# Feed-forward of a prompt and a sample group: the prompt in 512-column matmuls, the sample tokens as stationary operand in four column groups

## The chip, the cores and the metric

One Trainium2 chip, one of its cores. The metric is the device time of one launch in microseconds (us); the shown time before is the median of three runs.

## The reference, cut to what matters

Two groups of tokens run through the same two-layer trunk with the same weights: a prompt of 1024 tokens and 8 x 4 = 32 sample tokens. Each layer has a mixer (layer 0 convolutions, layer 1 attention) and then the feed-forward part, which is what the change touches (cut, with `D_MODEL` = 1024 and `D_FF` = 2816):

```python
def causal_dwconv(x, state, w):           # width 3; returns the last 2 input rows as new state
    xp = jnp.concatenate([state, x], axis=1)
    ...
def conv_ffn(h, st, w_in, wc, w_down):
    z = h @ w_in
    g, st_new = causal_dwconv(z[..., :D_FF], st, wc)
    return (jax.nn.silu(g) * z[..., D_FF:]) @ w_down, st_new
...
    fp, nfp = conv_ffn(rms_norm(hp, g_ffn[layer]), zf, w_ffn_in[layer], conv_f_w[layer], w_down[layer])
    fs, nfs = conv_ffn(rms_norm(hs, g_ffn[layer]), state_ffn[layer], w_ffn_in[layer], conv_f_w[layer], w_down[layer])
    hp = hp + fp
    hs = hs + fs
```

All data are fp32.

## The kernel before

Activations lie transposed: channels on the 128 partitions, tokens along the row, the 1024 prompt tokens first and the 32 sample tokens behind them (`T` = 1056). A matmul takes a 128x128 block of weights as stationary operand and streams tokens. The 1056 tokens are three pieces of 352 (`NT` = 3, `TS` = 352), each into a PSUM bank of its own; the two regions `reg[0]` and `reg[1]` have three banks each and alternate from use to use (`region(use)`).

Precision comes from splitting: every fp32 value is a rounded part (type fp32r, one pass of TensorE) and a rest. ScalarE makes the rounded part of a unit of weights (`split_hi`, line 381), GpSimd the rest (`split_lo`, line 386), and each product is taken as high*high, high*low, low*high. So one block of 128x128 weights against all tokens is 3 x 3 = 9 matmuls of 352 columns.

Weights come as a stream of units of 128x1024 values (512 KB). `w_raw` has three slots for what was loaded, `w_sp` three for the split parts. SyncE's queue loads unit u once `w_lo` says that the unit in the same slot, u-3, was split (`load_unit`, line 374); it also issues the copies of the caches (`copy_piece`, 4 MB each). The split of unit u+3 is made when TensorE has finished unit u (`hi_after`, `lo_after`).

The feed-forward part of a layer (`ffn(L)`) has 11 groups of 256 hidden channels. A group has four units of the input projection (gate and up of two chunks of 128 channels; `in_proj`, line 626, 72 matmuls a unit) and two units of the down projection (`down_proj`, line 677, 72 matmuls a unit in four uses of 18). The down projection of group g-1 stands behind the input units of group g. Its first two input units go with `first_units`, which puts between them the sums for the norm's factor: VectorE takes reciprocals (lines 1535 and 1537) into `rst`, with which every result of the input projection is multiplied when it leaves PSUM.

Per chunk the other engines work so: VectorE reads the gate from PSUM (line 1761), convolves the prompt (lines 1772, 1774) and the sample tokens (1784, 1786), ScalarE takes silu (1246), GpSimd multiplies by `rst` (1469), VectorE multiplies by the up part from PSUM (1795), ScalarE and VectorE split the result into `hid` (1249, 1750). After each use of the down projection VectorE adds the region to `h` (line 1553). Every engine has its own program in written order, with semaphores between them.

Sample attention in layer 1 uses another form, which the prediction reads: 32 columns of stationary operand (queries or probabilities of one sequence) against fp32 keys or values, four sequences one after the other into the four groups of 32 PSUM partitions (lines 979 and 992).

## Time and profile before

| what | value |
|---|---|
| median of 3 runs (lowest, highest) | 2667.09 us (2666.91, 2667.24) |
| span of the profiled execution, first to last instruction | 2666.3 us |
| TensorE (PE) busy | 2615.1 us, 98% of the span |
| VectorE (DVE) busy | 1386.6 us, 52% |
| ScalarE (ACT) busy | 632.3 us, 24% |
| GpSimd (POOL) busy | 659.3 us, 25% |
| mean granted TensorE clock | 0.996 of full speed |

The time of the profiled execution and its span differ by less than 1 us from the median of the runs. PE is the matmul part of TensorE and PEld its weight loads, which overlap matmuls. A matmul's record runs from its start to the modelled end of its last result, so consecutive records overlap; how long one takes in a stream is seen from the busy time of many divided by their number. A fp32 matmul (not fp32r) has two records.

### The profile page before, as it was taken

The page shows a single profiled execution, that of the slowest core. Times are in us where ns is not written, and L with a number is a line of the kernel's source. Part 1 is how long each engine was busy: PE and PEld are TensorE (multiplying, and loading weights), DVE is VectorE, ACT ScalarE, POOL GpSimd, SP SyncE. Part 2 cuts the span into 40 slices and gives each one's busy share as a digit, 9 for nine tenths or more (in the row PEclk, how much of TensorE's full clock was granted, in tenths as well). Part 3 has the DMA queues.
Part 4 walks back from the last instruction along what each step waited for, and adds up shares of the span by engine and source line. Part 5 has one row for each costly group of instructions (what it writes and reads, how often), then busy time and mean ns, then how long its engine had stood idle before and what let it go on. Part 6 is the DMA issues. An engine that isn't in the chain of part 4 may idle for free.

```text
span 2666.3 us, 41371 instructions
## 1 busy us (share of the span) xinstructions
PE 2615.1 (98%) x17564; PEld 2461.4 (92%) x17564; DVE 1386.6 (52%) x2023; ACT 632.3 (24%) x955; POOL 659.3 (25%) x388
## 2 busy tenths in 40 slices
PE   8999999999999999999999999989999999999997
PEld 8999999999999999987777777769999999999997
DVE  6999764443444444555565555552544444444444
ACT  5111332111111111233333333332311111111112
POOL 1000144332333223331010101123433323333332
PEclk9999999999999999999999999999999999999998
DMA  4111112333332433134344444446454444444411
GB/s 149 40 40 48 43 43 54 111 105 108 111 111 103 158 126 111 68 136 165 133 151 143 154 147 165 144 162 254 174 174 166 167 151 155 152 172 174 174 43 65
DMA packets 94008, 336.72 MB, mean 126 GB/s; under 512 B 22544, under 2 KB 39824, under 8 KB 91408
## 3 DMA queue, kind: packets, MB, share of 16 engines
q1 hardware_dynamic: 93840, 334.20, 36.6%
q8 instruction: 139, 2.28, 0.3%
q14 instruction: 29, 0.24, 0.0%
HBM read 315.88 MB, written 152.25 MB: 176 GB/s over the span
## 4 chain that ended last, share of the span: by engine, by line
PE 95%; DVE 3%; ACT 1%; issue 1%; DMA 0%; DVEq 0%; SPq 0%; ACTq 0%
PE reg L626 50%; PE reg L677 19%; PE reg L903 9%; PE reg L765 3%; PE reg L883 3%; PE ob L939 3%; PE reg L856 1%; PE reg L924 1%; PE ob L924 1%; PE reg L992 1%; PE reg L646 1%; PE reg L979 1%; DVE neg_s L1857 1%; DVE neg_s L1873 1%; PE ob L739 1%
## 5 line engine op out<-in xcount | busy, mean ns | idle before, releaser
L626 PE MATMUL reg<-xs,w_sp 128*128 128x352 f32 x8208 | 1338.8, 324 | 11.3 <-DVE xs L1542 11.0
L626 PEld LDWEIGHTS reg<-xs,w_sp 128*128 128x128 f32 x8208 | 1329.9, 188 | 16.1 <-issue 15.4
L386 POOL TENSOR_TENSOR w_sp<-w_raw,w_sp 128x1024 fp32r<-128x1024 f32 x152 | 370.3, 2437 | 1230.4 <-ACT w_sp L381 1208.3
L677 PE MATMUL reg<-hid,w_sp 128*128 128x352 f32 x3150 | 511.4, 323 | 0.0
L677 PEld LDWEIGHTS reg<-hid,w_sp 128*128 128x128 f32 x3150 | 508.6, 188 | 0.0
L381 ACT ACTIVATE w_sp<-w_raw 128x1024 fp32r<-128x1024 f32 x172 | 182.2, 1059 | 1046.8 <-PE reg L626 611.7
L1553 DVE TENSOR_TENSOR h<-reg,h 128x1056 f32<-128x1056 f32 x199 | 250.1, 1257 | 295.8 <-PE reg L677 233.5
L903 PE MATMUL reg<-xs,w_sp 128*128 128x352 f32 x1512 | 279.5, 332 | 0.4 <-DVE VT L1839 0.4
L1761 DVE TENSOR_TENSOR g<-reg,rst 128x1056 f32<-128x1056 f32 x44 | 55.4, 1259 | 415.1 <-PE reg L626 415.0
L903 PEld LDWEIGHTS reg<-xs,w_sp 128*128 128x128 f32 x1512 | 240.6, 188 | 18.1 <-issue 18.0
L404 POOL TENSOR_TENSOR w_sp<-w_raw,w_sp 128x1024 fp32r<-128x1024 f32 x21 | 50.0, 2382 | 475.8 <-ACT w_sp L399 457.0
L1469 POOL TENSOR_TENSOR sil<-sil,rst 128x1056 f32<-128x1056 f32 x44 | 90.5, 2057 | 217.1 <-ACT sil L1246 217.1
L1795 DVE TENSOR_TENSOR tmp<-reg,sil 128x1056 f32<-128x1056 f32 x44 | 55.3, 1258 | 151.3 <-POOL sil L1469 79.6
L1246 ACT ACTIVATE sil<-acc 128x1056 f32<-128x1056 f32 x44 | 47.9, 1089 | 342.2 <-DVE acc L1786 342.2
L1309 ACT ACTIVATE pT<-ob 128x512 f32<-128x512 f32 (+1 forms) x96 | 47.2, 492 | 328.9 <-PE ob L924 328.9
L1774 DVE SCALAR_TENSOR_TENSOR acc<-g,pt,acc 128x1024 f32<-128x1024 f32 x88 | 113.1, 1285 | 12.0 <-DVE acc L1772 1.5
L1857 DVE CUSTOM_DVE_ANT_0 neg_s<-reg,wt 128x512 f32<-128x512 f32 (+1 forms) x192 | 107.2, 558 | 6.6
L1302 ACT ACTIVATE neg_s<-neg_s,nmx 128x896 f32<-128x896 f32 (+7 forms) x128 | 98.1, 768 | 35.9 <-DVE nmx L1862 33.3
L1593 DVE SCALAR_TENSOR_TENSOR g<-g,pt,g 128x1024 f32<-128x1024 f32 x80 | 103.6, 1295 | 2.2
L1880 DVE COPY pT<-reg 128x512 f32<-128x512 f32 (+1 forms) x96 | 53.4, 556 | 97.6 <-PE reg L924 97.2
L1750 DVE TENSOR_TENSOR hid<-tmp,hid 128x1056 fp32r<-128x1056 f32 x44 | 100.3, 2280 | 2.3 <-ACT hid L1249 2.3
L765 PE MATMUL reg<-xs,w_sp 128*128 128x352 f32 x576 | 95.5, 325 | 0.3 <-DVE h L1553 0.3
(209 smaller groups left out, 1908.5 us busy)
## 6 DMA issues: line engine op xcount, KB each, us to landing
w_raw<-in_wstream SPq DMA_DIRECT2D x193, 512.0 KB, 3.6
out_sv<-in_cache_v SPq DMA_DIRECT2D x16, 4088.0 KB, 15.2
out_sk<-in_cache_k SPq DMA_DIRECT2D x16, 4088.0 KB, 15.4
kvr<-in_kva SPq DMA_DIRECT2D x16, 2048.0 KB, 8.9
kvr<-in_kvb SPq DMA_DIRECT2D x16, 1536.0 KB, 7.1
wt<-in_wtab SPq DMA_DIRECT2D x16, 512.0 KB, 5.0
h_spill<-h SPq DMA_DIRECT2D x8, 528.0 KB, 2.6
out_kT<-KT SPq DMA_DIRECT2D x8, 528.0 KB, 10.5
```

Source lines behind the costliest of these rows:

```text
L381: nc.scalar.activation(w_sp[:, u % 3, 0, :], w_raw[:, u % 3, :], ACT.Copy).then_inc(w_hi, 1)
L386: nc.gpsimd.tensor_tensor(w_sp[:, u % 3, 1, :], w_raw[:, u % 3, :], w_sp[:, u % 3, 0, :].bitcast(F32), ALU.subtract).then_inc(w_lo, 1)
L626: mm = nc.tensor.matmul(out[:, t, :], w[:, wh, k * P:(k + 1) * P], xs[:, xh, k, t * TS:(t + 1) * TS], start=(n == 0 and wh + xh == 0), sto ...
L677: mm = nc.tensor.matmul(out[:, t, :], w[:, wh, kk * 512 + m * P:kk * 512 + (m + 1) * P], hid[:, par_g, kk, xh, t * TS:(t + 1) * TS], start ...
L765: mm = nc.tensor.matmul(out[:, t, :], w[:, wh, (2 * k + m2) * P:(2 * k + m2 + 1) * P], xs[:, xh, place + k, t * TS:(t + 1) * TS], start=(k ...
L903: mm = nc.tensor.matmul(dense[:, t, :], w[:, wh, k * P:(k + 1) * P], xs[:, xh, k, t * TS:(t + 1) * TS], start=(k == 0 and wh + xh == 0), s ...
L1302: nc.scalar.activation(neg_s[:, hh, 0:w], neg_s[:, hh, 0:w], ACT.Exp, bias=nmx[:, m, hh:hh + 1], scale=-1.0, accum_out=lsum[:, 0, hh:hh + ...
L1553: nc.vector.tensor_tensor(tok(h[:, m, :]), region(r), tok(h[:, m, :]), ALU.add).then_inc(free, 1)
L1593: ins = nc.vector.scalar_tensor_tensor(out=y, in0=src, scalar=w, in1=y, op0=ALU.mult, op1=ALU.add)
L1750: nc.vector.tensor_tensor(hid[:, g % 2, c, 1, :], tmp[:, :], hid[:, g % 2, c, 0, :].bitcast(F32), ALU.subtract).then_inc(hid_lo, 1)
L1774: chain(nc.vector.scalar_tensor_tensor(out=y, in0=src, scalar=w, in1=y, op0=ALU.mult, op1=ALU.add))
L1857: nc.vector.tensor_tensor_reduce(out=neg_s[:, hh, lo:lo + w], in0=S[hh][:, 0:w], in1=wt[:, hh, t0:t0 + w], scale=-1.0, scalar=3.0e38, op0= ...
```

## The change

In the feed-forward parts of both layers the 1024 prompt tokens go through TensorE as two pieces of 512 in place of three of 352 (`wide_proj`, `down_proj`, `last_halves`); high and low parts as before. The 32 sample tokens leave this stream. Their normalised activations `xsn` (unsplit fp32, 32 tokens) become the stationary operand and the loaded weights `w_raw` (unsplit fp32) stream: `sample_pair` computes a gate unit and an up unit in 16 fp32 matmuls of 128 columns, into the four groups of 32 partitions (two units, and the eight blocks of the contraction in two halves). ScalarE copies the result to SBUF (`si_sb`), and `merge`, one fp32 matmul against `sel` (two identities), adds the halves and turns the result back to channels on partitions. `sample_down` does the down projection of a group in 8 fp32 matmuls of 256 columns, accumulated over all groups in one bank; `turn_down` turns it back at the end of the layer. VectorE reads the merged rows (`sample_rows`), multiplies the up part (`hid_s`) and adds the sample result to `h` once a layer. Since TensorE reads `w_raw` itself now, a slot is loaded again only when the sample matmuls have read it (`sample_read` in `load_unit`). The other engines' feed-forward instructions cover 1024 columns where the sample tokens went apart.

```diff
+        def sample_read(sp, v):
+            for L in range(2):
+                n = v - U_FFN[L]
+                if 0 <= n < 66:
+                    g, y = (0, n) if n < 4 else (1 + (n - 4) // 6, (n - 4) % 6)
+                    if n >= 64:
+                        sp.wait_ge(sd_done, NG * (L + 1))
+                    elif y >= 4:
+                        sp.wait_ge(sd_done, NG * L + g)
+                    else:
+                        sp.wait_ge(si_full, NJ * L + 2 * g + y // 2 + 1)
...
             if i is not None or u >= 3:
                 sp.wait_ge(w_lo, at(cnt(u) - 3, i, step))
+            sample_read(sp, u - 3)
...
+            def wide_proj(u, r, i=None, x_at=None, midway=None, mid_k=KD // 2):
...
+                for k in range(KD):
+                    if midway and k == mid_k:
+                        midway()
...
+                    for wh, xh in ((0, 0), (0, 1), (1, 0)):
+                        for t in range(2):
+                            mm = nc.tensor.matmul(out[:, t, :], w[:, wh, k * P:(k + 1) * P],
+                                                  xs[:, xh, k, t * 512:(t + 1) * 512],
+                                                  start=(k == 0 and wh + xh == 0), stop=(k == KD - 1 and wh == 1))
...
+            def sample_pair(L, j):
+                u = in_unit(L, j // 2, 2 * (j % 2))
+                raw_landed(u)
+                raw_landed(u + 1)
+                if j == 0:
+                    pe.wait_ge(xsn_ok, L + 1)
+                if j >= 2:
+                    pe.wait_ge(si_ok, NJ * L + j - 1)
+                for k4 in range(4):
+                    for x in range(2):
+                        for half in range(2):
+                            k, lo = 4 * half + k4, NS * (2 * x + half)
+                            mm = nc.tensor.matmul(SI[j % 2][lo:lo + NS, :], xsn[:, k, :],
+                                                  w_raw[:, (u + x) % 3, k * P:(k + 1) * P],
+                                                  start=(k4 == 0), stop=(k4 == 3))
+                mm.then_inc(si_full, 1)
+            def merge(L, j):
+                pe.wait_ge(si_ok, NJ * L + j + 1)
+                if j > 0:
+                    pe.wait_ge(sm_free, NJ * L + j)
+                nc.tensor.matmul(SM, si_sb[:, j % 2, :], sel[:, :],
+                                 start=True, stop=True).then_inc(sm_full, 1)
+            def sample_down(L, g):
...
+                pe.wait_ge(hid_s_ok, NJ * L + 2 * g + 2)
+                for kk in range(2):
+                    for j in range(4):
+                        c = kk * 512 + 2 * P * (j % 2)
+                        mm = nc.tensor.matmul(SD[NS * j:NS * (j + 1), :], hid_s[:, g % 2, kk, :],
+                                              w_raw[:, (u + j // 2) % 3, c:c + 2 * P],
+                                              start=(g == 0 and kk == 0), stop=(g == NG - 1 and kk == 1))
+                mm.then_inc(sd_done, 1)
...
+                for g in range(1, NG):
+                    for x in range(4):
+                        u = in_unit(L, g, x)
+                        wide_proj(u, FIRST[u], midway=(lambda: merge(L, 2 * g + x)) if x < 2 else None)
+                        if g == 1 and x == 0:
+                            sample_pair(L, 3)
+                        if x == 1:
+                            sample_down(L, g - 1)
+                    if g < NG - 1:
+                        sample_pair(L, 2 * g + 2)
+                    pe.wait_ge(hid_lo, NJ * L + 2 * g)
+                    for x in range(2):
+                        u = down_unit(L, g - 1, x)
+                        down_proj(u, FIRST[u], (g - 1) % 2)
+                        if g == NG - 1 and x == 0:
+                            sample_down(L, NG - 1)
+                    if g < NG - 1:
+                        sample_pair(L, 2 * g + 3)
...
+                chain(nc.vector.tensor_tensor(xsn[:, :, :], h[:, :, NP_:],
+                                              rst[:, NP_:].unsqueeze(1).to_broadcast([P, KD, NS]), ALU.mult))
```

TensorE's order in a group in the middle of a layer: one group of input units (lines 626 and 705) and the down units (677 and 733). Before:

```order
L626 MATMUL reg<-xs,w_sp 128x352 x288
L677 MATMUL reg<-hid,w_sp 128x352 x144
L626 MATMUL reg<-xs,w_sp 128x352 x288
L677 MATMUL reg<-hid,w_sp 128x352 x144
L626 MATMUL reg<-xs,w_sp 128x352 x288
```

After, from the last sample pair of the group ahead to the next one (line 756 is `sample_pair`, 766 `merge`, 778 `sample_down`; the names behind the arrow are operands):

```order
L756 MATMUL ob<-w_raw,xsn 32x128 x16
L705 MATMUL reg<-xs,w_sp 128x512 x24
L766 MATMUL reg<-sel,si_sb 128x64
L705 MATMUL reg<-xs,w_sp 128x512 x48
L766 MATMUL reg<-sel,si_sb 128x64
L705 MATMUL reg<-xs,w_sp 128x512 x24
L778 MATMUL ob<-w_raw,hid_s 32x256 x8
L705 MATMUL reg<-xs,w_sp 128x512 x96
L756 MATMUL reg<-w_raw,xsn 32x128 x16
L733 MATMUL reg<-hid,w_sp 128x512 x96
L756 MATMUL ob<-w_raw,xsn 32x128 x16
```

A group's 432 matmuls became 288, and five insertions stand between them: two pairs, two merges, one down.

VectorE's order at the start of a layer's feed-forward part, from the end of `new_x` to the first chunk. Before:

```order
L1542 SCALAR_TENSOR_TENSOR xs<-h,pt,xs 128x1056 x2
L1535 RECIPROCAL rst<-rst 128x1024
L1537 RECIPROCAL rst<-rst 128x32
L1761 TENSOR_TENSOR g_64<-reg,rst 128x1056
L1772 TENSOR_SCALAR acc<-g_64,pt 128x1024
L1774 SCALAR_TENSOR_TENSOR acc<-g_64,pt,acc 128x1024 x2
L1784 TENSOR_SCALAR acc<-sx,pt 128x32
L1786 SCALAR_TENSOR_TENSOR acc<-sx,pt,acc 128x32 x2
L1795 TENSOR_TENSOR tmp<-reg,sil 128x1056
```

After:

```order
L1669 SCALAR_TENSOR_TENSOR xs<-h,pt,xs 128x1056 x2
L1662 RECIPROCAL rst<-rst 128x1024
L1664 RECIPROCAL rst<-rst 128x32
L1878 TENSOR_TENSOR sel<-ident 128x64
L1881 TENSOR_TENSOR xsn<-h,rst 128x256
L1883 TENSOR_TENSOR xsn<-xsn,pt 128x256
L1911 TENSOR_TENSOR g_64<-reg,rst 128x1024
L1925 TENSOR_SCALAR acc<-g_64,pt 128x1024
L1927 SCALAR_TENSOR_TENSOR acc<-g_64,pt,acc 128x1024 x2
L1900 COPY sx<-reg 128x8x4
L1901 COPY up_s<-reg 128x32
```

Three instructions came between the reciprocals and the first read of the gate, and the two copies of the merged rows between the prompt's convolution and the sample tokens' one.

## Rows read from the trace of the kernel before

**Rows 1.** The page: engines, clock slices and the chain that ended last.

```profile
PE 2615.1 (98%) x17564; PEld 2461.4 (92%) x17564; DVE 1386.6 (52%) x2023; ACT 632.3 (24%) x955; POOL 659.3 (25%) x388
PEclk9999999999999999999999999999999999999998
PE 95%; DVE 3%; ACT 1%; issue 1%; DMA 0%; DVEq 0%; SPq 0%; ACTq 0%
PE reg L626 50%; PE reg L677 19%; PE reg L903 9%; PE reg L765 3%; PE reg L883 3%; PE ob L939 3%; PE reg L856 1%; PE reg L924 1%; PE ob L924 1%; PE reg L992 1%; PE reg L646 1%; PE reg L979 1%; DVE neg_s L1857 1%; DVE neg_s L1873 1%; PE ob L739 1%
```

**Rows 2.** TensorE's timeline, layer 0's feed-forward part: start, us, line, shapes, count.

```profile
371.10 12.06 PE L626 MATMUL reg<-xs,w_sp 128*128 128x352 f32 x72
382.99 1.88 PE L705 MATMUL ob<-acc,ones 128*128 128x512 f32 x4
466.46 23.39 PE L677 MATMUL reg<-hid,w_sp 128*128 128x352 f32 x144
489.69 46.73 PE L626 MATMUL reg<-xs,w_sp 128*128 128x352 f32 x288
536.26 23.39 PE L677 MATMUL reg<-hid,w_sp 128*128 128x352 f32 x144
...
1094.66 46.64 PE L677 MATMUL reg<-hid,w_sp 128*128 128x352 f32 x288
1141.14 1.13 PE L856 MATMUL reg<-xs,w_sp 128*128 128x352 f32 x6
```

**Rows 3.** Windows of 100 us in the feed-forward parts: PE busy (count), clock, DMA.

```profile
600.00:700.00 100.00, 100.00 (x621) 1.00 0.34 119
2000.00:2100.00 100.00, 100.00 (x621) 1.00 0.49 168
```

**Rows 4.** Timeline around a 512-column fp32 stretch in layer 0's mixer.

```profile
130.45 1.88 PE L739 MATMUL ob<-g,diag 128*128 128x512 f32 x4
```

**Rows 5.** Timeline: sample values in four groups between dense matmuls, 128 columns streamed.

```profile
1233.15 0.51 PEld L903 LDWEIGHTS reg<-xs,w_sp 128*128 128x128 f32 x3
1233.89 1.72 PEld L992 LDWEIGHTS reg<-kvr,spT 128*32 128x32 f32 x64 [0.23 <-issue]
1233.92 1.96 PE L992 MATMUL reg<-kvr,spT 128*32 128x128 f32 x64
1235.81 0.94 PEld L903 LDWEIGHTS reg<-xs,w_sp 128*128 128x128 f32 x6 [0.20 <-issue]
```

**Rows 6.** The same form with 24 records, and with 512 columns streamed.

```profile
1248.95 0.86 PE L992 MATMUL reg<-kvr,spT 128*32 128x128 f32 x24
1249.75 0.42 PE L998 MATMUL reg<-vnew,spT 32*32 32x128 f32 x8
...
1194.24 1.92 PE L979 MATMUL reg<-kvr,qb 128*32 128x512 f32 x16
1196.09 0.30 PEld L903 LDWEIGHTS reg<-xs,w_sp 128*128 128x128 f32 x2 [0.84 <-issue]
```

**Rows 7.** Timeline: one 32-column fp32 matmul, 128 stationary columns, inside the stream.

```profile
390.04 0.35 PEld L626 LDWEIGHTS reg<-xs,w_sp 128*128 128x128 f32 x2
390.37 0.35 PEld L710 LDWEIGHTS ob<-acc,ones 128*128 128x128 f32 x2
390.64 0.46 PEld L626 LDWEIGHTS reg<-xs,w_sp 128*128 128x128 f32 x3
```

**Rows 8.** Timeline: the other engines at the start of layer 0's feed-forward part.

```profile
386.77 6.55 DVE L1535 RECIPROCAL rst<-rst 128x1024 f32<-128x1024 f32 x1 [5.39 <-ACT rst L1097]
393.36 0.35 DVE L1537 RECIPROCAL rst<-rst 128x32 f32<-128x32 f32 x1
393.75 1.26 DVE L1761 TENSOR_TENSOR g<-reg,rst 128x1056 f32<-128x1056 f32 x1
396.17 2.60 DVE L1774 SCALAR_TENSOR_TENSOR acc<-g,pt,acc 128x1024 f32<-128x1024 f32 x2
400.83 2.06 POOL L1469 TENSOR_TENSOR sil<-sil,rst 128x1056 f32<-128x1056 f32 x1 [3.32 <-ACT sil L1246]
403.02 1.26 DVE L1795 TENSOR_TENSOR tmp<-reg,sil 128x1056 f32<-128x1056 f32 x1 [3.39 <-POOL sil L1469]
```

**Rows 9.** A middle unit: weight splits, and DMA issues with us to landing.

```profile
641.10 1.06 ACT L381 ACTIVATE w_sp<-w_raw 128x1024 fp32r<-128x1024 f32 x1 [10.55 <-PE reg L626]
642.23 2.40 POOL L386 TENSOR_TENSOR w_sp<-w_raw,w_sp 128x1024 fp32r<-128x1024 f32 x1 [9.22 <-ACT w_sp L381]
...
w_raw<-in_wstream SPq DMA_DIRECT2D x193, 512.0 KB, 3.6
out_sv<-in_cache_v SPq DMA_DIRECT2D x16, 4088.0 KB, 15.2
```

More of the change, by code:

```diff
@@ L196, in build @@
         M0 = off
-        hid, off = place("hid", [P, 2, 2, 2, T], F32R, off)
+        hid, _ = place("hid", [P, 2, 2, 2, NP_], F32R, off)
+        off += 2 * 2 * 2 * T * 4
         W0 = off
@@ L233, in build @@
         assert o2 <= SPARE0 + 4 * T
+        si_sb, o2 = place("si_sb", [P, 2, P], F32, PR0)
+        sel, o2 = place("sel", [P, 2 * NS], F32, o2)
+        hid_s, o2 = place("hid_s", [P, 2, 2, NS], F32, o2)
+        assert o2 <= PR0 + 4 * NB * (NQ // 2) * KA
+        xsn, o2 = place("xsn", [P, KD, NS], F32, M0 + 2 * 2 * 2 * NP_ * 4)
+        sd_sb, _ = place("sd_sb", [P, 2, P], F32, M0 + 2 * 2 * 2 * NP_ * 4)
+        assert o2 <= W0
+        up_s, o2 = place("up_s", [P, 2, NS], F32, off)
+        assert o2 <= nc.sbuf_usable_end
         g0, o2 = place("g0", [P, PAD + T], F32, M0)
@@ L652, in last_two, with last_halves @@
                             mm.then_inc(x_free, 1)
-            def last_thirds(w, out):
-                for t in range(NT):
+            def wide_proj(u, r, i=None, x_at=None, midway=None, mid_k=KD // 2):
+                pe.wait_ge(w_lo, at(cnt(u), i, 12))
+                open_use(r, i)
+                out, w = wide(r), w_sp[:, u % 3]
+                for k in range(KD):
+                    if midway and k == mid_k:
+                        midway()
+                    if x_at is not None:
+                        pe.wait_ge(x_lo, x_at + k + 1)
+                    for wh, xh in ((0, 0), (0, 1), (1, 0)):
[3 more added lines that the diff above has]
+                                                  start=(k == 0 and wh + xh == 0), stop=(k == KD - 1 and wh == 1))
+                mm.then_inc(full, 1)
+            def last_halves(w, out):
+                for t in range(2):
                     for kk in range(2):
@@ L669, in down_proj @@
                     open_use(r + m, i)
-                    out = region(r + m)
+                    out = wide(r + m)
                     if r + m == LAST_USE:
-                        last_thirds(w, out)
+                        last_halves(w, out)
                         return
@@ L682, in token_sums, with turn_down @@
+            def turn_down(L):
+                pe.wait_ge(sd_ok, L + 1)
+                for x in range(2):
+                    mm = nc.tensor.transpose(ST[:, x * P:(x + 1) * P], sd_sb[:, x, :], ident[:, :])
+                mm.then_inc(sdt_full, 1)
             def token_sums(src, blocks=range(NBLK)):
@@ L823, in ffn @@
                 first_units(s, (5, 9)[L], in_unit(L, 0, 0), e * KD)
+                sample_pair(L, 0)
                 for x in range(2, 4):
-                    in_proj(in_unit(L, 0, x), FIRST[in_unit(L, 0, x)])
-                def down(g, i):
-                    pe.wait_ge(hid_lo, at(NJ * L + 2 * g + 2, i, 4))
-                    for x in range(2):
-                        u = down_unit(L, g, x)
-                        down_proj(u, FIRST[u], g % 2, i)
-                for i in range((NG - 1) // 2):
-                    for g in (1, 2):
-                        for x in range(4):
-                            u = in_unit(L, g, x)
-                            in_proj(u, FIRST[u], i)
-                        down(g - 1, i)
-                down(NG - 1, None)
+                    u = in_unit(L, 0, x)
+                    wide_proj(u, FIRST[u], midway=lambda: merge(L, x - 2), mid_k=1)
+                    sample_pair(L, x - 1)
+                for g in range(1, NG):
[9 more added lines that the diff above has]
+                    pe.wait_ge(hid_lo, NJ * L + 2 * g)
+                    for x in range(2):
+                        u = down_unit(L, g - 1, x)
[4 more added lines that the diff above has]
+                        sample_pair(L, 2 * g + 3)
+                pe.wait_ge(hid_lo, NJ * (L + 1))
+                for x in range(2):
+                    u = down_unit(L, NG - 1, x)
+                    down_proj(u, FIRST[u], (NG - 1) % 2, behind_first=(lambda: turn_down(L)) if x == 0 else None)
             ffn(0)
@@ L1051, in _ @@
             ffn(1)
-            for t in range(NT):
+            for t in range(2):
                 pe.wait_ge(acc_third, t + 1)
-                mm = token_sums(acc, [j for j, lo in enumerate(BLOCKS) if t * TS < lo + P <= (t + 1) * TS])
+                mm = token_sums(acc, (range(4), range(4, NBLK))[t])
             mm.then_inc(tk_full, 1)
@@ L1255, in ffn @@
                         for c in range(2):
+                            sample_rows(g, c, i)
+                        for c in range(2):
                             chunk(g, c, i)
@@ L1745, in ffn @@
                 factor_parts((5, 9)[L])
+                turned = ident[:, :].rearrange("p (x s t) -> p x s t", x=2, s=2)
+                chain(nc.vector.tensor_tensor(sel[:, :].rearrange("p (x t) -> p x t", x=2), turned[:, :, 0, :],
+                                              turned[:, :, 1, :], ALU.add))
+                g0c = KD * (1, 3)[L]
+                chain(nc.vector.tensor_tensor(xsn[:, :, :], h[:, :, NP_:],
+                                              rst[:, NP_:].unsqueeze(1).to_broadcast([P, KD, NS]), ALU.mult))
+                nc.vector.tensor_tensor(xsn[:, :, :], xsn[:, :, :],
+                                        pt[:, g0c:g0c + KD].unsqueeze(2).to_broadcast([P, KD, NS]),
+                                        ALU.mult).then_inc(xsn_ok, 1)
                 def hidden_lo(g, c, i):
```

125 lines of the change are left out of this document (86 added, 39 removed).

## The prediction

> **What bounds the kernel now.** I read the page first, for who is busy and who ends last. TensorE is busy for 98% of the span, 95% of the chain that ended last is its own work, and no other engine is above 52%; the clock row shows full speed up to the last slice [rows 1]. So only TensorE's stream counts. The timeline of layer 0's feed-forward part shows it without a hole: 288 input matmuls from 489.69 to 536.26, 161.7 ns each; 144 down matmuls from 466.46 to 489.69, 161.3 ns [rows 2]. One group of six units is 69.80 us (466.46 to 536.26), and every group of both layers is made of the same 432 matmuls. The windows in both layers say the same: 621 records touch each 100 us, two of them only by their edges, which is 161.6 ns, at a granted clock of 1.00, the 2.4 GHz level, whatever the DMA queues do (0.34 and 0.49 busy) [rows 3]. 22 groups are 22 x 69.80 = 1535.6 us, 58% of the time. The question is what the stream costs afterwards.
>
> 352 columns at 2.4 GHz are 146.7 ns. The stream takes 161.6. Those 15 ns of excess are what the change lives from, and whether they come once a matmul or with every column decides it. That is the first unknown. A fp32 stream has nothing like it: four records of 512 columns take 1.88 us with a modelled tail of 0.16 (as 466.46 + 23.39 overlaps 489.69), that is 430 ns for a record of two passes, 215 ns for 512 columns [rows 2, 4].
>
> **What the change removes.** 132 units x 72 = 9504 matmuls of 352 columns become 132 x 48 = 6336 of 512. If the excess comes once a matmul, one takes 213.3 + 15.0 = 228.3 ns; 6336 of them are 1446.5 us, and 89.1 us are saved. If it comes with the columns, one takes 161.6 x 512/352 = 235.1 ns, in sum 1489.3 us, and only the sample tokens' 3% of columns go: 46.3 us. If it is gone at 512, as in the fp32 row, 215 ns give 1362.2 us and 173.4 us. Nearest to the new matmuls are the old ones of the same type (rounded fp32, each with its own weight load). I take the excess once a matmul: VectorE and DMA traffic leave the rate as it is, and a start that a stream at full reading rate can't hide is the simplest reading of a fp32 stream that reads at half that rate and has no excess. It is a reading and not shown.
>
> **What it adds on TensorE.** Nearest rows are those of sample attention, the same shapes: 32 stationary columns, fp32, four partition groups in turn.
> - A block in groups. 64 records take 1.89 us (1233.92 to 1235.81) and 24 take 0.80, so one costs 27.3 ns [rows 5, 6]. A fp32 matmul is two records, and 128 columns twice are 107 ns: four groups really run at once. The first dense load ahead starts 0.19 before 1233.66, the next dense load comes at 1235.81, 2.34 us later where 0.16 is normal, and the six loads there are 0.06 us closer than in a stream: the block costs the stream 2.12 us. 1.75 of it are the 64 records and 0.37 is the way into the groups and back.
> - `sample_pair`: 32 records x 27.3 ns + 0.37 = 1.24 us; 44 of them are 54.7 us.
> - `sample_down`: 16 records of 512 columns take 1.85 us to the next dense load, 0.14 of it fixed as above, so 107 ns a record and 53 for 256 columns [rows 6]. 16 x 53 ns + 0.37 = 1.22 us; 22 of them are 26.9 us.
> - `merge`: the nearest is the one matmul of 32 columns with a full stationary operand in the middle of a unit. The dense load behind it comes 0.27 us later, the two after it 0.05 us closer: 0.22 us, two weight loads of 0.11, which 64 columns don't lengthen [rows 7]. 44 are 9.7 us.
> - `turn_down`: two transposes a layer, about 0.5 us in all by the same row.
>
> That is 91.8 us, against 89.1 saved.
>
> **What it adds elsewhere.** VectorE, ScalarE and GpSimd do 3% less per chunk, and get small copies and products of 32 tokens; they have room [rows 1]. The two places where they could bind are these.
>
> The start of a layer. VectorE's reciprocals end at 393.71 and the gate is read at 393.75 [rows 8]. Now `sel` and `xsn` come between, by the rows for 32 and for 1024 columns (0.35 and 1.30 us) some 0.1 + 2 x 0.4 us in all, so `xsn` is there at about 394.6. TensorE ends the second input unit at 384.2 + 48 x 0.228 + 0.22 = 395.4. `sample_pair(L, 0)` doesn't wait, nor does the unit behind it, whose region is read until 395.8. But the load of the fourth unit, and all behind it on SyncE's queue, waits for that pair now, to 396.6; before, it hung only on the split of the first unit, which is made a unit ahead. Then come 3.6 us to landing, 1.06 + 2.40 for the split [rows 9], 2.06 for GpSimd's product behind it, 1.26 for VectorE's read that empties the region [rows 8]: 407.2, where TensorE wants region and weights at 396.6 + 11.2 + 1.2 = 409.0. 1.8 us of slack, in both layers. If that cover is gone, TensorE waits for what is over. The first unit of layer 0 waits for its inputs already (382.99 - 371.10 = 11.89 us for 11.65 of work) [rows 2] and will not get shorter by its full share; I add 0.5 us.
>
> The middle. Splits take 3.5 us after each unit's end [rows 9], then 3.6 for a load, or at worst 15.2 more behind a whole cache copy [rows 9]; the sample matmuls want that unit two units (22 us) later. SyncE's new waits are for pairs and downs that lie earlier still. The merges wait for ScalarE's copies, half a unit behind the pair. I cost these at nothing. They lie beside units of 11 us.
>
> Sum: 2666.3 - 89.1 + 91.8 + 0.5 = 2669.5 for the profiled execution's span, 2670 for the median, which stands 0.8 above it. **The forecast is 2670 us**, no change that can be told: within 0.2% (5.3 us) is about what a measurement of this kernel can tell from nothing. Balance lies at (1535.6 - 92.3) / 6336 = 227.8 ns a matmul, and 5.3 us are 0.84 ns of it. So even in the likeliest case all three signs are open.
>
> **The rivals.**
> - *The excess once a matmul, near 15 ns* (the forecast): 224 to 232 ns by alignment and start, 2643 to 2694 us. Chance 0.55, of it 0.20 faster, 0.22 same, 0.13 slower.
> - *The excess goes with the columns*, 235.1 ns: 2667 - 46.3 + 92.3 = 2713 us, slower. For it: 15 ns on 147 in a type that reads twice the bytes in a nanosecond that the fp32 stream reads. Against: nothing in these rows, since all rounded matmuls are of 352 columns. It decides from 228.6 ns upwards. Chance 0.22. The Trainium skill, "SBUF — State Buffer", in its note on cachelines, says that a read wants at least two hits in each line of 16 bytes to hide the latency; with 4-byte values a line is left after four columns, so by it a loss would grow with the columns. No row here shows a line.
> - *The excess is gone at 512*, 215 ns: 2667 - 173.4 + 92.3 = 2586 us, faster by 3%. For it the fp32 stream [rows 4]; against it that this stream has twice the time per column to fetch. Chance 0.17. The Trainium skill, "TensorE: Matmul & The Clock Gate", section on the back-to-back issue gap, gives columns / 2.4 GHz + 2.5 ns; for 352 columns that is 149.2 ns, and the trace's 161.6 disagrees. For 512 it would be 215.8 ns and the sum 2591 us.
> - *The late loads at a layer's start bind*: the slack of 1.8 us is gone if loads land later than 5.4 us, as behind a cache copy of layer 1 (15.2 us [rows 9]), or if the split meets VectorE on the same data. Price some 5 us a layer, 2680. Chance 0.04.
> - *The four groups do not overlap* with weights streaming and 16 matmuls in a row: each pair 2.6 us more, each down 2.6, 172 us in all, 2842 us. [rows 5, 6] speak against it. Chance 0.02.
>
> **How the numbers follow.** Faster: 0.20 + 0.17 and a hundredth for cheaper insertions = 0.38. Same: 0.22. Slower: 0.13 + 0.22 + 0.04 + 0.02 with rounding = 0.40. The range takes the likeliest case whole, the case of the columns to its end (2713 and a few us of waits, 2718), and below goes half way to the 215 ns, to 2620 (220 ns a matmul); what is beneath, some 0.13, and above, 0.05, is left out.
>
> **What the profile will show.** The rate of the 512-column matmuls in a group's middle: 228 ns if I am right, 235 or 215 by the rivals; it decides more than all else. A group of 288 matmuls should take 65.75 us + 2 x 1.24 + 2 x 0.22 + 1.22 = 69.9 us, against 69.80. A pair's 32 records about 0.87 us, a down's 16 about 0.85, each with 0.37 around it; four matmuls starting together show the groups at work. No waits of TensorE on ScalarE, VectorE or DMA in the middle, and at most 1 us at `xsn` or behind the fourth unit of a layer. Wrong would be the forecast by 6.3 us for every nanosecond by which the rate is not 228, and by 0.66 us for every 10 ns in the way into and out of the groups.

## The result, and the profile after

| | before | changed |
|---|---|---|
| time, median | 2667.07 us | 2721.14 us (2718.58 to 2724.64, 4 runs) |
| ratio | | 1.020, interval 1.019 to 1.022 |
| profiled execution: span | 2666.3 us | 2716.8 us |
| mean granted TensorE clock | 0.996 | 0.994 |

The change costs 54 us, 2.0%. The forecast was 2670, the range 2620 to 2718. The four executions lie 6 us apart, the longest at the lowest mean clock (0.991); the profiled one is the shortest. The engines' row and the clock row of the page after, to be read beside [rows 1]:

```profile
PE 2635.3 (97%) x16248; PEld 2167.6 (80%) x16248; DVE 1433.4 (53%) x2161; ACT 638.8 (24%) x1000; POOL 627.1 (23%) x302
PEclk9999999999999999999999999999999999999998
```

No engine but TensorE is near its limit, as before. TensorE has fewer instructions, is busy 20 us longer and idle 30 us more. By stage, from the first and last dense matmul of each, the span's 50.5 us are +26.4 in layer 0's feed-forward part (369.0 to 1165.3; before 371.1 to 1141.0), +24.3 in layer 1's, and nearly nothing elsewhere. TensorE's timeline for one group (start, us, line, count), to be read beside [rows 2]:

```profile
544.07 1.08 PE L756 MATMUL reg<-w_raw,xsn 128*32 128x128 f32 x32
545.08 3.02 PE L733 MATMUL reg<-hid,w_sp 128*128 128x512 f32 x12
549.12 19.35 PE L733 MATMUL reg<-hid,w_sp 128*128 128x512 f32 x84 [1.02 <-DVE tmp L1953]
...
575.06 0.33 PE L766 MATMUL reg<-sel,si_sb 128*128 128x64 f32 x2
575.20 11.30 PE L705 MATMUL reg<-xs,w_sp 128*128 128x512 f32 x48
586.34 0.33 PE L766 MATMUL reg<-sel,si_sb 128*128 128x64 f32 x2
...
592.18 1.07 PE L778 MATMUL ob<-w_raw,hid_s 128*32 128x256 f32 x16
593.19 22.40 PE L705 MATMUL reg<-xs,w_sp 128*128 128x512 f32 x96
615.52 1.08 PE L756 MATMUL reg<-w_raw,xsn 128*32 128x128 f32 x32
```

The group takes 71.45 us (544.07 to 615.52) where 69.9 were forecast and 69.80 stood before. 1.02 us of it is a hole that was not there: TensorE waits for the second region of the down projection. L756 is a sample pair, 1.01 to the next dense matmul; L778 a down, 1.01; L766 a merge, 0.14 to the next start. The hole costs more than its 1.02, since a wait is counted from the modelled end of the matmul ahead: that one starts at 547.71 (548.10 less its 0.39), the next at 549.12, so 1.41 us lie between two starts where 0.23 is normal, and the cost is 1.18. The list of waits gives the hole's sum (us in total, times, longest), and the list of groups by form has the other half in L705:

```profile
PE reg L733 <- DVE tmp L1953: 23.6, 20, 2.2
L705 PE MATMUL reg<-xs,w_sp 128*128 128x512 f32 x4224 | 1002.2, 396 | 7.2 <-DVE tmp L1953 6.8 <-DVE xs L1669 0.4
```

So TensorE waits 23.6 + 6.8 = 30.4 us for `tmp`, VectorE's product that empties the region of an up unit. VectorE's and GpSimd's timelines at this place:

```profile
543.53 2.00 POOL L1593 TENSOR_TENSOR sil<-sil,rst 128x1024 f32<-128x1024 f32 x1 [5.76 <-ACT sil L1371]
545.48 2.40 POOL L423 TENSOR_TENSOR w_sp<-w_raw,w_sp 128x1024 fp32r<-128x1024 f32 x1
545.73 2.20 DVE L1951 TENSOR_TENSOR hid_s<-up_s,sil 128x32 f32<-128x32 f32 x1 [3.40 <-POOL sil L1593]
547.86 1.21 DVE L1953 TENSOR_TENSOR tmp<-reg,sil 128x1024 f32<-128x1024 f32 x1
...
521.00 0.19 DVE L1951 TENSOR_TENSOR hid_s<-up_s,sil 128x32 f32<-128x32 f32 x1 [3.40 <-PE reg L705]
521.11 1.22 DVE L1953 TENSOR_TENSOR tmp<-reg,sil 128x1024 f32<-128x1024 f32 x1
```

`hid_s`, the product of 32 sample columns, stands ahead of `tmp`. One of its 44 lasts 0.19 us at 521.00, where GpSimd does nothing, and the next 2.20 at 545.73, where GpSimd's split of a weight unit has just begun; it ends as the split ends. 22 of the 44 are like the one and 22 like the other. `tmp` comes 2 us late, and TensorE waits for the part of it that other work doesn't cover.

The other new hole is 3.32 us at 410.90, at the fourth input unit of layer 0 (3.47 in layer 1). GpSimd, ScalarE and VectorE there:

```profile
398.85 1.06 ACT L418 ACTIVATE w_sp<-w_raw 128x1024 fp32r<-128x1024 f32 x1 [3.44 <-DMA w_raw<-in_wstream]
399.99 2.40 POOL L423 TENSOR_TENSOR w_sp<-w_raw,w_sp 128x1024 fp32r<-128x1024 f32 x1 [21.77 <-ACT w_sp L418]
402.33 0.51 POOL L1585 COPY sx<-sf_st 128x352 f32<-128x352 f32 x1
402.93 0.19 DVE L1900 COPY sx<-reg 128x32 f32<-128x32 f32 x1 [6.27 <-POOL sx L1585]
405.27 2.00 POOL L1593 TENSOR_TENSOR sil<-sil,rst 128x1024 f32<-128x1024 f32 x1 [2.18 <-ACT sil L1371]
407.40 2.21 DVE L1951 TENSOR_TENSOR hid_s<-up_s,sil 128x32 f32<-128x32 f32 x1 [3.33 <-POOL sil L1593]
409.54 1.21 DVE L1953 TENSOR_TENSOR tmp<-reg,sil 128x1024 f32<-128x1024 f32 x1
```

The load behind the first pair lands as forecast and its split ends at 402.4. But GpSimd's copy of the convolution history into `sx` stands behind that split in its program, and VectorE waits 6.27 us for it. `tmp` is done at 410.75; the forecast had 407.2, with the region wanted at 409.0. It was wanted at 407.5.

After most of the longer waits the clock falls. Windows of 1 us behind the hole at 410.90 (the window's length, busy time of PE, PEld, DVE, ACT and POOL, the granted clock, then the share of DMA and its GB/s):

```profile
412.00:413.00 1.00, 1.00 (x6) 0.80 (x4) 1.00 (x2) 0.96 (x2) 0.00 (x0) 0.52 1.26 193
413.00:414.00 1.00, 1.00 (x4) 0.81 (x4) 1.00 (x2) 0.00 (x0) 0.96 (x1) 0.50 0.79 43
...
415.00:416.00 1.00, 1.00 (x4) 0.79 (x4) 0.98 (x1) 0.00 (x0) 1.00 (x2) 0.78 0.00 0
```

TensorE had idled 3.32 us and had just started again when the clock went to the 1.2 GHz level, for 3.4 us. That happens four times: here, in the last group of layer 0 (a hole of 2.2 us), in attention, and at layer 1's start (a hole of 3.47 us). It is no rule for each hole: in the last group of layer 1 TensorE waits the same 2.2 us, up to 2649.5, and the clock stays at 1.00 until 2690. Windows of 33 us through the whole span show 0.95, 0.95, 0.95 and 0.90 there and 0.99 or more elsewhere ahead of the tail, so up to 33 x 0.25 = 8.3 us are lost (TensorE idles in part of them, 1.4 us in the one at layer 1's start); before there is no such window.

### The profile page after: what moved, and what is told of

It is laid out like the page before. It is cut to its first block and busy times, and to the rows that moved or that the text cites. A ratio compares the mean times of both kernels' runs of the same rounds, so it can differ in the third digit from the quotient of the medians.

```text
span 2716.8 us, 38988 instructions
## 1 busy us (share of the span) xinstructions
PE 2635.3 (97%) x16248; PEld 2167.6 (80%) x16248; DVE 1433.4 (53%) x2161; ACT 638.8 (24%) x1000; POOL 627.1 (23%) x302
## 5 line engine op out<-in xcount | busy, mean ns | idle before, releaser
L705 PE MATMUL reg<-xs,w_sp 128*128 128x512 f32 x4224 | 1002.2, 396 | 7.2 <-DVE tmp L1953 6.8
L705 PEld LDWEIGHTS reg<-xs,w_sp 128*128 128x128 f32 x4224 | 788.5, 188 | 195.0 <-issue 21.6
L733 PE MATMUL reg<-hid,w_sp 128*128 128x512 f32 x2100 | 491.0, 393 | 23.7 <-DVE tmp L1953 23.6
L733 PEld LDWEIGHTS reg<-hid,w_sp 128*128 128x128 f32 x2100 | 392.0, 188 | 117.6 <-DVE tmp L1953 32.0
L1680 DVE TENSOR_TENSOR h<-reg,h 128x1024 f32<-128x1024 f32 x175 | 214.3, 1224 | 208.7 <-PE reg L733 206.6
L664 PE MATMUL reg<-xs,w_sp 128*128 128x352 f32 x1872 | 308.7, 326 | 10.1 <-DVE xs L1669 9.7
L664 PEld LDWEIGHTS reg<-xs,w_sp 128*128 128x128 f32 x1872 | 304.4, 189 | 13.4 <-issue 13.0
L1911 DVE TENSOR_TENSOR g<-reg,rst 128x1024 f32<-128x1024 f32 x44 | 53.9, 1225 | 437.9 <-PE reg L705 437.7
L1021 PE MATMUL reg<-xs,w_sp 128*128 128x352 f32 x1512 | 279.6, 332 | 0.4 <-DVE VT L2003 0.4
L1021 PEld LDWEIGHTS reg<-xs,w_sp 128*128 128x128 f32 x1512 | 240.6, 188 | 18.1 <-issue 18.0
L1593 POOL TENSOR_TENSOR sil<-sil,rst 128x1024 f32<-128x1024 f32 x44 | 88.0, 2000 | 229.4 <-ACT sil L1371 229.4
L1951 DVE TENSOR_TENSOR hid_s<-up_s,sil 128x32 f32<-128x32 f32 x44 | 52.6, 1195 | 153.7 <-PE reg L705 78.9
```

Source lines behind the costliest of these rows:

```text
L664: mm = nc.tensor.matmul(out[:, t, :], w[:, wh, k * P:(k + 1) * P], xs[:, xh, k, t * TS:(t + 1) * TS], start=(n == 0 and wh + xh == 0), sto ...
L705: mm = nc.tensor.matmul(out[:, t, :], w[:, wh, k * P:(k + 1) * P], xs[:, xh, k, t * 512:(t + 1) * 512], start=(k == 0 and wh + xh == 0), s ...
L733: mm = nc.tensor.matmul(out[:, t, :], w[:, wh, kk * 512 + m * P:kk * 512 + (m + 1) * P], hid[:, par_g, kk, xh, t * 512:(t + 1) * 512], sta ...
L1021: mm = nc.tensor.matmul(dense[:, t, :], w[:, wh, k * P:(k + 1) * P], xs[:, xh, k, t * TS:(t + 1) * TS], start=(k == 0 and wh + xh == 0), s ...
L1593: nc.gpsimd.tensor_tensor(sil[:, PAD:PAD + NP_], sil[:, PAD:PAD + NP_], rst[:, 0:NP_], ALU.mult).then_inc(silr_ok, 1)
L1680: nc.vector.tensor_tensor(halves(h[:, m, 0:NP_]), wide(r), halves(h[:, m, 0:NP_]), ALU.add).then_inc(free, 1)
```

## The experiments

Theory: the 54 us over the kernel before are two waits of program order, with the clock that they cost, on top of a rate and of insertions that about cancel. Rivals: the loads are late; the excess of a matmul over its columns' time grows with the columns; VectorE loses the time wherever the product stands.

**Runs 1 and 2: take `hid_s` from ahead of `tmp`.**

```diff
 e1_swap, VectorE's chunk:
+nc.vector.tensor_tensor(halves(tmp[:, 0:NP_]), wide(ru), halves(sil[:, PAD:PAD + NP_]), ALU.mult).then_inc(free, 1)
 nc.vector.tensor_tensor(hid_s[:, g % 2, c, :], up_s[:, c, :], sil[:, PAD + NP_:], ALU.mult).then_inc(hid_s_ok, 1)
-nc.vector.tensor_tensor(halves(tmp[:, 0:NP_]), wide(ru), halves(sil[:, PAD:PAD + NP_]), ALU.mult).then_inc(free, 1)

 e2_gpsimd, GpSimd's chunk, ahead of its own product (the line is gone from VectorE's):
+pool.wait_ge(sm_free, at(j + 1, i, 4))
+nc.gpsimd.tensor_tensor(hid_s[:, g % 2, c, :], up_s[:, c, :], sil[:, PAD + NP_:], ALU.mult).then_inc(hid_s_ok, 1)
```

> Changed kernel with one edit: in VectorE's chunk the product of 32 sample columns (hid_s) stands behind the product that empties the region (tmp), not ahead of it. Theory A (hid_s takes 2.2 us instead of 0.19 where it meets GpSimd's split of a weight unit, and what stands behind it, tmp, frees the region late): TensorE's waits for tmp at the second region of a down projection, 23.7 us in 22 groups, go to under 2 us, the wait at each layer's start falls from 3.4 to about 1.3 us, and the granted clock no longer falls there. That is 24 + 4 + some 4 = 32 us, 2689 us. hid_s itself is still 2.2 us where it meets the split. Rival B (the region is late because GpSimd's product or the load behind it is late, and hid_s only shows that wait): the waits stay at 1.0 to 1.4 us, the time within 5 us of 2721. Rival C (VectorE loses the same 2 us wherever it stands, to whatever two-operand product meets the split): tmp takes 2 us more and the time stays, 2721.

> Changed kernel with hid_s computed on GpSimd, just ahead of its own product of the chunk, instead of on VectorE. On one engine it can't meet the split. Theory A: as in the run with the two VectorE products exchanged, the 23.7 us of waits in the groups go; GpSimd's product starts some 0.2 to 0.5 us later, which the groups cover (tmp waited for by nobody then), but not the layer's start, whose wait is 3.4 - 2.1 + 0.3 = 1.6 us. About 2690 us. Rival B (VectorE is held by GpSimd's load on SBUF as such): some other product of VectorE grows to 2.2 us, and 2715 to 2725 us stay.

Measured: 2684.25 us (ratio to before 1.006, 1.005 to 1.008) and 2684.42 (the same interval). 36.9 us come back, 32 were expected. VectorE and GpSimd in e1_swap:

```profile
518.65 2.41 POOL L423 TENSOR_TENSOR w_sp<-w_raw,w_sp 128x1024 fp32r<-128x1024 f32 x1 [1.20 <-ACT w_sp L418]
518.79 2.31 DVE L1953 TENSOR_TENSOR hid_s<-up_s,sil 128x32 f32<-128x32 f32 x1
...
542.15 2.40 POOL L423 TENSOR_TENSOR w_sp<-w_raw,w_sp 128x1024 fp32r<-128x1024 f32 x1
542.39 1.23 DVE L1951 TENSOR_TENSOR tmp<-reg,sil 128x1024 f32<-128x1024 f32 x1 [3.40 <-POOL sil L1593]
543.53 1.07 DVE L1953 TENSOR_TENSOR hid_s<-up_s,sil 128x32 f32<-128x32 f32 x1
```

`hid_s` now meets the split nearly every time, and ends with it whether it began 0.1 us into it (2.31) or 1.4 us (1.07). `tmp`, which reads PSUM and SBUF, runs through the same split in 1.23 as ever. So rival C falls: it is not any product that loses the time, but this one, with both its operands in SBUF. The Trainium skill, "SBUF — State Buffer", section "SBUF: two separate sides", says that of a VectorE operation with two SBUF inputs and a GpSimd operation that reads SBUF the one that starts first holds a shared port pair for its whole instruction, and the other waits. The trace agrees: `hid_s` ends 0.05 us behind the split each time.

The kernel before shows the same meeting, in the product that makes the low part of `hid` from two operands in SBUF. VectorE and GpSimd there:

```profile
525.94 2.39 POOL L386 TENSOR_TENSOR w_sp<-w_raw,w_sp 128x1024 fp32r<-128x1024 f32 x1 [9.24 <-ACT w_sp L381]
525.98 3.46 DVE L1750 TENSOR_TENSOR hid<-tmp,hid 128x1056 fp32r<-128x1056 f32 x1
...
540.51 1.25 DVE L1750 TENSOR_TENSOR hid<-tmp,hid 128x1056 fp32r<-128x1056 f32 x1
```

It takes 1.25 us alone and 3.46 where the split has just begun, ending 1.11 us behind the split, so nearly its whole length lies there. 20 of its 44 are like that. TensorE waited for none of them, but the price of such a meeting could be read before the change.

TensorE's waits at L733 are no longer among those of 0.2 us and more, and at L705 2.7 us are left. One wait is new: 1.5 us of a merge for `si_sb`, in layer 1's second group (run 9 is about it). The clock falls once, in attention (0.90 in one window, 3.3 us); why it falls there is open. 30.4 - 2.7 - 1.5 = 26.2 us of waits, 3.2 for the 0.16 that each of 20 holes costs over its listed wait, and 8.3 - 3.3 = 5.0 of clock make 34.4, against 33.9 between the two profiled spans. e2_gpsimd has `hid_s` in 0.24 us on GpSimd, the same time, and 60 us less on VectorE, which nobody waited for.

**Run 3: the rate by width.**

```diff
 wide_proj and down_proj:
-for t in range(2): out[:, t, :], t * 512 : (t + 1) * 512
+for t, lo, n in PIECES[layer]: out[:, t, lo:lo + n], t * 512 + lo : t * 512 + lo + n
```

> Changed kernel with narrower matmuls: layer 0's feed-forward matmuls in four pieces of 256 columns, layer 1's in pieces of 384 and 128. It asks how the time over columns / 2.4 GHz grows: 15 ns at 352 and 14 to 17 at 512 so far. Excess once a matmul (my reading): 256 columns 106.7 + 15.5 = 122 ns, 384 columns 160.0 + 15.5 = 175.5 ns, 128 columns 53.3 + 15.5 = 69 ns. Excess with the columns (4.6 percent and more): 111.6, 167.4 and 55.8 ns; or a weight load of its own length (0.11 us by the rows of single weight loads) bounds the 128-column one from below. By the first, layer 0's 66 units take 66 x 48 x (2 x 122 - 229.5) = 46 us more than in the changed kernel, layer 1's 66 x 48 x (175.5 + 69 - 229.5) = 47.5 us, and the time is 2815 us; by the second 2700 us.

Measured: 2900.79 us (one execution). TensorE's timeline, 192 matmuls of 256 columns in layer 0's down units (with the next row's start), and 96 pairs of 384 and 128 in layer 1's:

```profile
526.11 23.09 PE L706 MATMUL reg<-xs,w_sp 128*128 128x256 f32 x192
549.12 1.08 PE L757 MATMUL reg<-w_raw,xsn 128*32 128x128 f32 x32
...
2126.59 27.73 PE L734 MATMUL reg<-hid,w_sp 128*128 128x384 f32 x192
2154.26 1.08 PE L757 MATMUL ob<-w_raw,xsn 128*32 128x128 f32 x32
```

(The first row is two input units.) 23.01 / 192 = 119.8 ns for 256 columns, an excess of 13.1; with the columns it would be 111.6. So the excess comes once a matmul, each with its own weight load: 13 ns at 256, 15 at 352, 14 at 512 in down units and 17 in input units (227.4 and 230.5 ns, run 4 is about the difference). Where it comes from stays open. My number for layer 1 was far off: a pair of 384 and 128 takes 27.67 / 96 = 288 ns and not 244.5. What fits is the bound named beforehand, a weight load of its own length for the short one: 175.5 + 110 = 286 ns. The starts of layer 1's weight loads agree, 178 and 108 ns apart in turn (medians): 178 is near what a 384-column matmul was to take, 108 the price of a single load, where a matmul of 128 columns was to take 69. 44 ns on 3168 pairs are the 140 us that I hadn't expected. The whole is only 86 us over the 2815, since layer 0 took 14 us less than expected, and the waits for `tmp` fell from 30.4 to 12.4 us; some 15 to 20 us of this sum are not placed.

**Run 4: the row's start.** (Input matmuls read some rows 32 tokens later, so the output is another.)

```diff
-xs[:, xh, k, t * 512:(t + 1) * 512]
+xs[:, xh, k, t * 512 + late(u, k):(t + 1) * 512 + late(u, k)]   # 32 for odd k in layer 0, for even k in layer 1
```

> Changed kernel in which the input matmuls read some rows of the prompt 32 columns (128 bytes) later: in layer 0 the odd blocks of features, in layer 1 the even ones. Rows of xs lie 4224 bytes apart, 16.5 times 256, so in layer 0 all blocks now start at the same place within 256 bytes as the even ones do, and in layer 1 all as the odd ones do. The input matmuls of those blocks read a window of tokens that is 32 later, so the output differs. Theory P (the odd start costs the input matmuls their 3 ns over the down matmuls, 230.5 against 227.4): layer 0's input units run at 227 ns, layer 1's at 234. 2112 matmuls a layer: the total stays near 2721, and the two layers differ by 15 us. Rival Q (the 3 ns are due to something else of input units, such as the wider spread of rows or writes of VectorE to xs): both layers stay at 230.5.

Measured: 2717.03 us (one execution). The middle 48 matmuls of a merge-to-merge stretch in layer 0, and 96 in layer 1, with the row that follows:

```profile
575.60 11.15 PE L709 MATMUL reg<-xs,w_sp 128*128 128x512 f32 x48
586.59 0.33 PE L770 MATMUL reg<-sel,si_sb 128*128 128x64 f32 x2
...
2119.28 22.56 PE L709 MATMUL reg<-xs,w_sp 128*128 128x512 f32 x96
2141.78 1.08 PE L760 MATMUL reg<-w_raw,xsn 128*32 128x128 f32 x32
```

10.99 us for 48 where the changed kernel has 11.14 (575.20 to 586.34): 3.1 ns a matmul less. 22.50 for 96 where it has 22.33: 1.8 ns more. All intervals inside the units say 227.2 in layer 0 and 232.4 in layer 1, against 230.5 in both and 227.4 for down matmuls. So P holds in layer 0 to its size; in layer 1 it has the sign, with half the size (1.8 to 1.9 ns for 3.5).

**Run 5: the history copy first.**

```diff
 GpSimd's chunk:
+if g == 0 and c == 0: (waits) nc.gpsimd.tensor_copy(sx[:, :, :, 0:KF - 1], sf_st[:]).then_inc(g_chain, 1)
 lo_after(pool, ug, i)
 pool.wait_ge(free, A.use(FIRST[ug] + 1))
-if g == 0 and c == 0: (waits) nc.gpsimd.tensor_copy(sx[:, :, :, 0:KF - 1], sf_st[:]).then_inc(g_chain, 1)
```

> The kernel with hid_s on GpSimd, and GpSimd's history copy (sx from sf_st) of each layer now ahead of the split of the second input unit in its program, not behind it. Theory D (the wait at the start of a layer is one of program order: VectorE's sample convolution needs that copy, and the copy stood behind a split whose unit had not landed): VectorE no longer waits 6.3 us for it, the SiLU comes at about 400, tmp at about 406, and TensorE's remaining wait of 1.4 us at the fourth input unit of each layer is gone. 2 x 1.4 = 2.8 us less than the 2684.4 of that kernel: 2681.5 us. Rival E (the load behind the first pair is what is late, by its wait for that pair): the split of the fourth unit is then itself too late, and 1.0 to 1.4 us a layer stay: 2684.

Measured: 2681.26 us, 3.2 less than e2_gpsimd. VectorE and TensorE at layer 0's start:

```profile
397.17 0.19 DVE L1903 COPY sx<-reg 128x32 f32<-128x32 f32 x1 [0.32 <-PE reg L766]
...
405.15 1.23 DVE L1954 TENSOR_TENSOR tmp<-reg,sil 128x1024 f32<-128x1024 f32 x1 [6.84 <-POOL sil L1596]
...
406.69 1.08 PE L756 MATMUL ob<-w_raw,xsn 128*32 128x128 f32 x32
407.71 1.66 PE L705 MATMUL reg<-xs,w_sp 128*128 128x512 f32 x6
```

The sample rows are read 5.8 us earlier than in the changed kernel (6.5 than in e2_gpsimd), `tmp` ends at 406.38, and the fourth unit starts behind its pair without a hole. GpSimd's product still stands behind the split that ends at 402.75, so the slack is 1.3 us, near the 1.8 forecast. Rival E falls. That the time met the expectation within 0.3 us is partly luck: the merge's wait for `si_sb` in layer 1 grew from 1.4 to 2.0 us, and the clock is low for 3.4 us where it was for 6.8.

**Run 6: aligned rows.**

```diff
+def prompt_row(x, m):
+    lo = NS * (m % 2)
+    return xs[:, x, m, lo:lo + NP_]
 wide_proj:
-xs[:, xh, k, t * 512:(t + 1) * 512]
+prompt_row(xh, k)[:, t * 512:(t + 1) * 512]
 gain_hi and gain_lo of the feed-forward parts write prompt_row(x, m) from h[:, m, 0:NP_]
```

> The kernel of e5_history, in which the feed-forward parts keep the prompt columns of the odd rows of xs 32 columns (128 bytes) further on, so that all 16 rows of 1024 columns start at the same place within 256 bytes; the sample columns of xs are not written there, since nothing of these parts reads them. Nothing is left out. Theory P (the start of the row is what the input matmuls pay for): input units at 227.5 instead of 230.5 to 231 ns in both layers, 4224 x 3.3 = 14 us less than e5_history, 2667.5 us. Also 3 percent off the writes of xs. Rival Q (the gain seen in layer 0 came from reading other data or from its neighbourhood): 2681.5 as before.

Measured: 2669.09 us, ratio 1.0006 (0.9997 to 1.0015): 12.2 us less, for 14 expected. A group is 69.51 us (536.31 to 605.82), under the 69.80 before. Input units run at 227.2 to 227.3 ns, down units at 227.0. Of the 1.8 us that are missing, 1.5 can be the same merge's wait, now 3.5 us.

**Run 7: the small work twice.** (A second merge in layer 0, second passes of each pair in layer 1, which write the same values again.)

```diff
-for k4 in range(4):
+for k4 in (range(4), [0, 1, 2, 3] * 2)[L]:
 merge:
+for n in range(2 - L):
```

> The kernel of e6_rows, with TensorE's small work done twice where it stands: in layer 0 each merge (one matmul of 64 columns more, 22 of them), in layer 1 each sample pair (16 matmuls more without leaving the column groups, 22 of them). It prices the parts of an insertion. If a pair is 32 records of 27.3 ns in four groups that run at once, and 0.34 us into the groups and back, layer 1 grows by 22 x 0.87 = 19.2 us; if the 64 more records cost their own weight loads (0.11 us each set of four) or the groups do not overlap, by 22 x 1.5 = 33 us or more. A second merge costs 0.11 us (its two passes of 64 columns and loads side by side with the first's) and not the whole 0.20: layer 0 grows by 2.4 us against 4.4. Sum: 2667.5 + 19.2 + 2.4 = 2689 us.

Measured: 2693.65 us (one execution). Rows of a merge stretch in layer 0 and of a pair in layer 1:

```profile
567.85 0.56 PE L771 MATMUL reg<-sel,si_sb 128*128 128x64 f32 x4
568.21 11.14 PE L709 MATMUL reg<-xs,w_sp 128*128 128x512 f32 x48
...
2122.73 1.96 PE L760 MATMUL reg<-w_raw,xsn 128*32 128x128 f32 x64
2124.61 22.05 PE L737 MATMUL reg<-hid,w_sp 128*128 128x512 f32 x96
```

A pair's second half costs 1.88 - 1.01 = 0.87 us, 22 of them 19.1, as by the first reading: four groups at once. The second merge costs 0.36 - 0.15 = 0.21 us, its whole price again and not the 0.11 I gave it. So the price of a merge comes with each merge, and breaking the stream adds little.

**Run 8: merges elsewhere.** What was expected still rests on the 0.11 that run 7 refutes.

```diff
-wide_proj(u, FIRST[u], midway=(lambda: merge(L, 2 * g + x)) if x < 2 else None)
+if x == 0: merge(L, 2 * g)
+wide_proj(u, FIRST[u])
+if x == 1: merge(L, 2 * g + 1)      # and then sample_down(L, g - 1)
```

> The kernel of e6_rows, with the merges of a group moved out of the middle of the input units to places where the dense stream is broken anyway: the first behind the sample pair that ends a group, the second ahead of sample_down. 40 of 44 merges are moved. If what an insertion costs is mostly the breaking of the dense stream (two exposed weight loads of about 0.11), each moved merge costs 0.11 us instead of 0.20, and 40 x 0.09 = 3.6 us are saved: 2664 us, a little under the kernel before. If the merge's own two passes with their loads cost the same anywhere, the time is that of e6_rows within 1 us, 2667.5. A wait of TensorE for ScalarE's copy of the pair just done would cost up to 1 us in each group, 2690; it should not come, since the merge behind a pair takes the rows of the pair before.

Measured: 2682.66 us (1.006, 1.005 to 1.007), 13.6 slower than e6_rows. Nothing is saved, by run 7's reason: a group takes 69.78 us (539.65 to 609.43), 0.30 of it a new hole, against 69.51. And the wait that I said should not come comes. ScalarE and TensorE behind a pair, and the longest wait:

```profile
562.75 1.06 ACT L422 ACTIVATE w_sp<-w_raw 128x1024 fp32r<-128x1024 f32 x1 [9.81 <-PE reg L737]
563.72 0.26 ACT L1372 ACTIVATE si_sb<-reg 128x128 f32<-128x128 f32 x1
...
564.03 0.43 PE L770 MATMUL reg<-sel,si_sb 128*128 128x64 f32 x2 [0.30 <-DVE h L1699]
...
1934.17 0.69 PE L770 MATMUL reg<-sel,si_sb 128*128 128x64 f32 x2 [9.00 <-ACT si_sb L1372]
```

The pair's rows were ready 23 us before, but ScalarE's copy of them stands behind its split of the second down unit, which waits for TensorE. That is 0.3 us in each of 18 groups, 5.4 us, and 1.9 and 9.0 us in the second groups of the two layers. The 9.0 are the wait that was 3.5 in e6_rows, met earlier. So 12.8 us of waits are new, against 11.5 between the two profiled spans. (The profile puts the small ones down to `h`; the copy ends at 563.98.)

**Run 9: cache copies elsewhere.**

```diff
-elif u >= 45 and u % 5 == 0:
+elif 44 <= u < 92 and u % 4 == 0:
     copy_piece(*pieces.pop())
-if u % 3 == 2 and pieces:
+if u % 3 == 2 and pieces and not U_FFN[1] <= u < U_FFN[1] + 9:
     copy_piece(*pieces.pop())
```

> The kernel of e6_rows (2669.1), with SyncE's copies of the caches placed elsewhere: none between the loads of layer 1's first nine feed-forward units, two more in layer 0's part. The same bytes are moved. In e6_rows TensorE waits once for 3.5 us at the first merge of layer 1's second group, since ScalarE's copy for it stands behind the split of a unit whose load, behind two cache copies of 4 MB, landed some 15 us after its issue. If that is the cause the wait goes, and what it takes from the clock with it: 3 to 6 us less, 2664.5 us, which would be 0.1 percent under the kernel before, hardly to be told from it. If the load is late without the copies too, 2669.

Measured: 2664.68 us (2663.86 to 2666.6, 11 runs), ratio 0.9991 (0.9982 to 1.0000). It removes this of e6_rows:

```profile
1926.64 1.06 ACT L422 ACTIVATE w_sp<-w_raw 128x1024 fp32r<-128x1024 f32 x1 [10.36 <-DMA w_raw<-in_wstream]
...
1928.86 0.58 PE L770 MATMUL reg<-sel,si_sb 128*128 128x64 f32 x2 [3.50 <-ACT si_sb L1369]
...
1930.00:1931.00 1.00, 1.00 (x3) 0.76 (x3) 1.00 (x1) 0.00 (x0) 0.13 (x1) 0.50 0.94 327
```

It is 56 us below the changed kernel, and 2.4 us below the one before, which this measurement can't tell from none. So late loads do count, once the other waits are gone: this wait is 1.4 to 3.5 us in runs 1, 2 and 5 to 7 and 9.0 in run 8. The changed kernel doesn't show it; it waits for 3.47 us at the unit ahead.

## Why the prediction was wrong

- **The balance** (89.1 saved against 91.8 added) was right in kind. The excess comes once a matmul (run 3). Mis-sized was its term: (4224 x 230.5 + 2112 x 227.4) / 6336 = 229.5 ns stand where 228.3 were taken, 7.4 us. The 3.1 ns of input units are the row's start (runs 4 and 6); without them the rate would have been 227.2. The rival with the columns, 235.1, is out; so is the one without excess, 215.
- **The insertions** were right: pair 1.21, down 1.20, merge 0.20 by the timeline, 88.4 us for 91.8. By run 7 a second merge of 64 columns costs 0.21 us, so the 0.22 read from one of 32 columns was right.
- **The failed step** is "I cost these at nothing", with "VectorE, ScalarE and GpSimd do 3% less per chunk, and get small copies and products of 32 tokens; they have room". They have room on the average. I priced a product of 32 columns by its length and not by what stands behind it or what runs beside it. It takes 2.2 us instead of 0.19 in half the chunks, ahead of the product that frees the region; 23.6 us in the groups. The list of what the profile would show said "No waits of TensorE on ScalarE, VectorE or DMA in the middle", and the list of waits refutes it.
- **The start of a layer**: the chain from pair to load to split was right, the slack of 1.8 us was not (its terms add up to 407.0, not 407.2, which changes little), since I left out GpSimd's history copy, which is queued behind that split and which VectorE now needs earlier in its chunk than any effect that I had listed. With `hid_s` it made 6.8 us in two layers. Run 5 gives the slack back, 1.3 us. The rival of late loads behind a cache copy, chance 0.04, was right about layer 1 in a place of its own: the merge of its second group, which run 9 frees.
- **The clock** was nowhere in the sum. Four drops, three of them behind new waits, cost up to 8.3 us, over a quarter of the waits themselves. What the clock did in attention, where no wait is new, is not explained.
- Sum for the span: 2669.5 + 30.4 (waits as listed) + 3.4 (what the holes cost beyond: 0.16 for 20 of them, 0.08 for the two behind pairs) + 8.3 (clock) + 7.4 (rate) - 3.4 (insertions) = 2715.6 for 2716.8; 1 to 2 us I can't place. The same calculation leaves more for run 9: by groups (69.51 against 69.80) it should be 6.4 us under the kernel before, and it is 2.4 to 3. Some 2 of these 4 us are small holes that the kernel before hasn't (0.5 us for `tmp` in the last group of each layer, 0.7 for it at layer 1's start, 0.5 in layer 0's first unit); the rest is open.

The repaired version shows where the expected gain went. 89 to 96 us are saved by fewer matmuls, and 88 of them go into the sample tokens' own work; what was left to win was a few us, and any small wait eats it.
